# A two-block transformer kernel on one core: eight more modulation blocks are summed by VectorE, and output chunks are put ahead of the last transposings

## The reference

```python
m_lat = (jax.nn.silu(c) @ ada_w[i] + ada_b[i])[:, None, :]      # ada_w[i]: 1024 x 6144
m_ctx = jax.nn.silu(c_ctx) @ ada_w[i] + ada_b[i]
sh1, sc1, g1, sh2, sc2, g2 = jnp.split(m_lat, 6, axis=-1)
h = _rms(x, norm1_g[i]) * (1.0 + sc1) + sh1
o, oc = _even_mixer(h, hc, ...)      # in-projection, Fourier mix, window attention, out-projection
x = x + g1 * o
h = _rms(x, norm2_g[i]) * (1.0 + sc2) + sh2
x = x + g2 * _swiglu(h, ffn_w_gate[i], ffn_w_up[i], ffn_w_down[i])
```

## Time and profile before

| | us |
|---|---|
| median of 3 runs | 2134.99 (2134.18 to 2138.87) |
| the profiled execution | 2134.16 |
| its span in the profile | 2132.3 |
| PE busy in the span | 2070.2 (97%) |
| DVE busy | 1499.5 (70%) |
| ACT busy | 975.3 (46%) |
| POOL busy | 325.4 (15%) |

### The profile page before, as it was taken

How to read it: one execution, slowest core, us unless ns; L and a number is a source line. 1 busy time by engine, 2 the same in 40 slices (tenths; PEclk the granted TensorE clock), 3 DMA queues, 4 the chain that set the end, 5 groups by cost and what they waited for, 6 DMA issues and landing times.

```text
span 2132.3 us, 34735 instructions
## 1 busy us (share of the span) xinstructions
PE 2070.2 (97%) x12633; PEld 1770.0 (83%) x12633; DVE 1499.5 (70%) x2685; ACT 975.3 (46%) x1545; POOL 325.4 (15%) x340
## 2 busy tenths in 40 slices
PE   7999999999989998999999999999999999999998
PEld 3756778888878768999999989999988888888887
DVE  5535578894247855665687867997986677777776
ACT  3436332222234365444478534447743444444444
POOL 0114000000004031000000016887820000000000
PEclk9999999999999999999999999999999999999999
DMA  8351245694226303555545544551156655555553
GB/s 294 118 210 69 99 158 194 214 325 136 96 79 179 99 11 110 186 180 188 181 160 165 174 159 136 172 169 60 60 184 221 198 187 188 190 191 189 187 188 117
DMA packets 92896, 342.18 MB, mean 160 GB/s; under 512 B 10383, under 2 KB 10399, under 8 KB 92272
## 3 DMA queue, kind: packets, MB, share of 16 engines
q1 hardware_dynamic: 89280, 325.10, 45.5%
q0 software_dynamic: 3504, 15.56, 2.5%
HBM read 339.57 MB, written 1.05 MB: 160 GB/s over the span
## 4 chain that ended last, share of the span: by engine, by line
PE 91%; DVE 4%; ACT 2%; issue 1%; DMA 1%; POOL 1%; SPq 0%; DVEq 0%; ACTq 0%; POOLq 0%
PE banks L1077 20%; PE banks L1514 16%; PE banks L1126 9%; PE banks L1480 7%; PE banks L1392 6%; PE banks L1263 5%; PE banks L1483 3%; PE banks L1441 3%; PE banks L975 2%; PE banks L1425 2%; PE banks L1091 2%; PE banks L1165 2%; PE banks L957 1%; PE banks L1004 1%; PE banks L1018 1%
## 5 line engine op out<-in xcount | busy, mean ns | idle before, releaser
L1077 PE MATMUL banks<-act_parts,first_w_parts 128*128 128x512 f32 (+1 forms) x2544 | 464.4, 344 | 3.1 <-DVE ffn_hidden_parts L2121 1.7
L1077 PEld LDWEIGHTS banks<-act_parts,first_w_parts 128*128 128x128 f32 x2544 | 400.9, 190 | 63.9 <-issue 7.3
L1514 PE MATMUL banks<-w_parts,a_parts 128*128 128x512 f32 x1524 | 360.4, 390 | 0.1
L2121 DVE TENSOR_TENSOR first_w_parts<-weight_ring,first_w_parts 128x1024 fp32r<-128x1024 f32 x166 | 206.8, 1248 | 202.1 <-ACT first_w_parts L1708 202.0
L1514 PEld LDWEIGHTS banks<-w_parts,a_parts 128*128 128x128 f32 x1524 | 285.9, 188 | 59.5 <-issue 0.8
L2121 DVE TENSOR_TENSOR w_parts<-weight_ring,w_parts 128x1024 fp32r<-128x1024 f32 x207 | 253.7, 1226 | 74.3 <-ACT w_parts L1708 71.7
L1708 ACT ACTIVATE w_parts<-weight_ring 128x1024 fp32r<-128x1024 f32 x207 | 218.9, 1057 | 184.0 <-PE banks L1480 102.1
L1708 ACT ACTIVATE first_w_parts<-weight_ring 128x1024 fp32r<-128x1024 f32 x166 | 174.8, 1056 | 237.2 <-PE banks L1077 124.0
L1480 PE MATMUL banks<-n_parts,w_parts 128*128 128x512 f32 x632 | 229.4, 397 | 1.3 <-DVE w_parts L2121 1.3
L1126 PE MATMUL banks<-ffn_hidden_parts,first_w_parts 128*128 128x512 f32 (+1 forms) x1056 | 183.4, 336 | 0.0
L1126 PEld LDWEIGHTS banks<-ffn_hidden_parts,first_w_parts 128*128 128x128 f32 x1056 | 162.6, 190 | 20.5
(11 more groups left out here) (327 smaller groups left out, 2904.0 us busy)
## 6 DMA issues: line engine op xcount, KB each, us to landing
weight_ring<-in_stream SPq DMA_DIRECT2D x618, 512.0 KB, 3.3
main_zone<-in_rel_bias POOLq DMA_DIRECT2D x6, 512.0 KB, 11.7
rounded<-in_dft_input POOLq DMA_DIRECT2D x1, 1600.0 KB, 7.5
rounded<-in_dft_inverse POOLq DMA_DIRECT2D x1, 1280.0 KB, 7.8
main_zone<-in_xT POOLq DMA_DIRECT2D x1, 1024.0 KB, 11.5
main_zone<-in_ctxT POOLq DMA_DIRECT2D x1, 1024.0 KB, 16.2
main_zone<-in_c_rows POOLq DMA_DIRECT2D x1, 1024.0 KB, 8.4
tail_zone<-in_rel_bias POOLq DMA_DIRECT2D x2, 512.0 KB, 23.6
```

What stands on the lines that cost most here:

```text
L1077: mm = pe.matmul(o[:, 0:w], wb[:, hw, k, :], fin[:, hx, k, 0:w], start=(k == 0 and n == 0), stop=(k == DC - 1 and n == 2))
L1514: mm = pe.matmul(acc[n][:, :], ap_[:, e % 3, ha, (n // 2) * P:(n // 2 + 1) * P], wp[(B + b) % PARTS][:, hw, (n % 2) * 512:(n % 2 + 1) * 51 ...
L2121: return dve.tensor_tensor(o, a, b, op)
```

## The change

Row 4 of layer 0 moves from TensorE to VectorE. Its eight blocks (`MODS` 0 to 7, two samples each) are summed by `mod_sums` inside `qk_norm`: blocks 0 to 3 after the last normalised chunk and before the first sine product, blocks 4 to 7 one before each later sine product. `SOONER` places their loads among those of `ada0b`, which now has 16 blocks. The condition rows for them are two new loads by GpSimd, and two SiLU by ScalarE after the last square root of `qk_root`. TensorE does 3, 2 and 1 `ada` blocks around the filter products instead of 6, 1 and 1, the same ten in turns 3 to 7, and none in the attention. ScalarE's `ada_copy(1)` stands before the attention instead of in its fourth step. In both attentions `out_part` comes before `turn` in the last steps, with more chunks in each. All of SP's loads of this part are written out instead of partly looped.

```diff
-STREAM = [("ada0a", 16), ("ev_in", 10), ("ada0b", 24), ("ev_out", 8), ("ffn_gu0", 2 * FC), ("mods", 56), ...
+STREAM = [("ada0a", 16), ("ev_in", 10), ("ada0b", 16), ("ev_out", 8), ("ffn_gu0", 2 * FC), ("mods", 64), ...
-MODS = ([(0, 5, _j, 2) for _j in range(8)] + ...
+MODS = ([(0, 4, _j, 2) for _j in range(8)] + [(0, 5, _j, 2) for _j in range(8)] + ...
+SOONER = {5: (0, 1), 7: (2,), 9: (3,), 11: (4,), 13: (5,), 15: (6, 7)}
-_at = 0
+_at = 8
...
         ORDER.append((_n, _i))
+        if _n == "ada0b":
+            ORDER += [("mods", _b) for _b in SOONER.get(_i, ())]
...
+        c_sooner = [second_rows[:, D:2 * D], view(CSOON0, D)]
...
-                if KIND[last + 1][0]:
+                if KIND[last + 1][0] and name != "ada0b":
                     return tile_free, TILE[name] + dict(TILES)[name]
                 return blocks_used, n + 2
...
-            fill = [[(1, "ada0b", b, b // DC, b // DC == 0, b // DC == 2) for b in range(24)], []]
+            fill = [[(1, "ada0b", b, b // DC, b // DC == 0, b // DC == 1) for b in range(16)], []]
...
-                for f in fill[0][:6]:
+                for f in fill[0][:3]:
                     ada(*f)
                 filter_dft(0)
-                ada(*fill[0][6])
+                for f in fill[0][3:5]:
+                    ada(*f)
                 filter_dft(1)
-                ada(*fill[0][7])
+                ada(*fill[0][5])
...
-                        for f in fill[0][2 * u + 2:2 * u + 4]:
+                        for f in fill[0][2 * u:2 * u + 2]:
                             ada(*f)
...
+                    if i >= PAIRS:
+                        out_part(l, AHEAD_OF_VALUES[l][i - PAIRS])
                     if 0 <= i - 2 < PAIRS:
                         turn(i - 2)
-                    if i >= PAIRS:
-                        out_part(l, AHEAD_OF_VALUES[l][i - PAIRS])
...
-            AHEAD_OF_VALUES = [[(0,), (1,), (2,)], [(0,), (1, 2), (3,)]]
+            AHEAD_OF_VALUES = [[(0,), (1, 2), (3, 4)], [(0,), (1, 2, 3), (4, 5)]]
...
-                    if l == 0 and i == 3:
-                        ada_copy(1)
...
             qk_root(0, 4)
+            act.wait_ge(crow_in, 32)
+            for s in (1, 0):
+                act.activation(c_sooner[s], c_sooner[s], ACT.Silu).then_inc(crow_ready, 1)
             dft_copy(0)
...
             v_copy()
+            ada_copy(1)
             attention(0)
...
                         if b == 0:
-                            dve.wait_ge(crow_ready, 2 - n)
+                            dve.wait_ge(crow_ready, 2)
+                            dve.wait_ge(dft_ready, 2)
+                        if b == 8:
+                            dve.wait_ge(crow_ready, 4 - n)
+                        o, c = (view(CPROD0, D), c_sooner[1 - n]) if b < 8 else (twins[3][:, :], c_rows[:, 1 - n, :])
...
+                mod_sums(range(4))
                 for j, (c, w, g, sq_at, r_at) in enumerate(CHUNKS[0]):
+                    if j >= 1:
+                        mod_sums([3 + j])
                     dve.wait_ge(rot_ready, j + 1)
...
+            pool.dma_start(c_sooner[0], t["c_rows"][:, 0:D]).then_inc(crow_in, 16)
...
+            pool.wait_ge(filt_ready, 6)
+            pool.dma_start(c_sooner[1], t["c_rows"][:, D:2 * D]).then_inc(crow_in, 16)
```

More of the change, by code:

```diff
@@ L60 @@
 GROUP = 2
-STREAM = [("ada0a", 16), ("ev_in", 10), ("ada0b", 24), ("ev_out", 8), ("ffn_gu0", 2 * FC), ("mods", 56), ("ffn_d0", FC),
+STREAM = [("ada0a", 16), ("ev_in", 10), ("ada0b", 16), ("ev_out", 8), ("ffn_gu0", 2 * FC), ("mods", 64), ("ffn_d0", FC),
           ("od_in", 24), ("od_out", 8), ("ffn_gu1", 2 * FC), ("ffn_d1", FC),
@@ L67 @@
           ("peer", 2 * KEYS - DONE)]
-MODS = ([(0, 5, _j, 2) for _j in range(8)] + [(1, _r, _j, 2) for _r in range(2) for _j in range(8)]
+MODS = ([(0, 4, _j, 2) for _j in range(8)] + [(0, 5, _j, 2) for _j in range(8)] + [(1, _r, _j, 2) for _r in range(2) for _j in range(8)]
         + [(1, _r, _j, 1) for _r in range(2, 6) for _j in range(8)])
 MODS_AT = {}
-_at = 0
+SOONER = {5: (0, 1), 7: (2,), 9: (3,), 11: (4,), 13: (5,), 15: (6, 7)}
+_at = 8
 for _m in range(1, 20):
@@ L255 @@
 CROWS0 = 21504
+CSOON0, CPROD0 = 25600, 19456
 HALF0 = FS0 + 2048
@@ L688, in release @@
                     return extra_ready, i + 1
-                if name in ("ada0a", "ada0b") and KIND[last + 1][0]:
+                if name in ("ada0a", "ada0b") and i == dict(STREAM)[name] - 1:
                     return ada_rows, 1 + ("ada0a", "ada0b").index(name)
-                if KIND[last + 1][0]:
+                if KIND[last + 1][0] and name != "ada0b":
                     return tile_free, TILE[name] + dict(TILES)[name]
@@ L792, in ada_turn @@
             def ada_turn(phase):
[L794 removed]
+                nj = 2
                 pe.wait_ge(ada_rows_copied, 2 * (phase + 1))
```

17 lines of the change are left out of this document (9 added, 8 removed).

## The result

| | before | with the change |
|---|---|---|
| median of 6 runs each, us | 2136.1 (2134.18 to 2139.2) | 2146.77 (2143.84 to 2155.79) |
| ratio, 95% interval | | 1.0051, 1.0039 to 1.0062 |
| profiled execution, span | 2134.16, 2132.3 | 2148.81, 2146.9 |

The kernel is slower by 10.7 us, where 4.8 was forecast. The direction was right (it had a chance of 0.50, against 0.46 for no change), the size was not: 2146.77 is above the range, which ended at 2143.0.

What follows compares the result with a forecast made beforehand. TensorE, 91% of the chain, was taken as the bound, with VectorE's late sums delaying the attention. +5.4 - 1.0 - 0.7 - 0.2 + 1.3 = +4.8 us took the median from 2134.99 to 2139.8, range 2134.5 to 2143.0.

Steps and rivals of the forecast that it cites:

- Prelude, -0.8: Fourier stage, filter products: fewer TensorE blocks around them, so turn 0 starts 0.8 us earlier, at 116.0 instead of 116.78.
- Ring: Fourier stage: blocks arrive through one ring in order, so VectorE's sums land late and rotations of chunks 2 and 4 wait.
- Lock, "nothing on the sum": First VectorE sum: locked beside GpSimd's cosine product, it takes about 6.6 us, adding nothing to the total.
- The last landings: End of Fourier stage: m6 lands at 145.2, VectorE's addition ends at 154.7, attention opens at 155.5 after 4.0 us idle TensorE.
- The stage's term: Fourier stage to first scores: attention opens at 155.5 instead of 150.09, +5.4 us, between -0.8 and about +8.
- Out-projection, -0.7 and -0.2: Ends of both attentions: out-projection chunks fill waits at the transposings, -0.7 us in the first, -0.2 in the second.
- Attention without fill, -1.0: First attention's start: without ada blocks the transposing ends at 157.0, saving 1.0 us, bounds 0 and 1.58.
- the clock, +1.3: First attention: the 4.0 us wait before it brings a fall of TensorE's clock, +1.3 us, between 0 and 2.6.
- At nothing: SiLU with table load, two GpSimd loads, ada_copy(1) and one more small addition: costed at nothing.
- At no term at all: Start of the program to the Fourier stage: the prediction had no term for it, forecast 0.
- two falls of the clock: Rival, Fourier turns 4 and 5: stalls lower the clock, delaying a10 and a12, 3 us more, 2143; chance 0.12.
- VectorE keeps up: Rival, Fourier stage: m3 lands by 129.0, VectorE is as early as TensorE, -2.7 us, 2132.3; chance 0.11.

Runs made afterwards that it cites:

- 2: The change without row 4's eight loads, VectorE making its sixteen full sums from data already in SBUF (row 4 not computed): 2136.75 us, ratio 1.0000.
- 3: The change without early sums and without their loads, one small copy instead (row 4 not computed): 2136.88 us, ratio 1.0004 to the kernel before.
- Experiment 8: The change with GpSimd's cosine product delayed until three blocks are summed: one run, 2142.78 us.
- 7: The kernel before with only the out-projection's part: out_part ahead of turn and the new AHEAD_OF_VALUES: 2137.43 us, ratio 1.0007.
- 6: The change with the unused matmuls of 4 and the useless fill of 5, row 4 computed: one run, 2141.71 us.
- 5: As 3, with six blocks' worth of useless 32-column matmuls in the attention's first three steps: 2137.4 us, ratio 1.0006 to the kernel before.
- 4: The change with four unused fp32 matmuls on TensorE after the turning of the values: 2144.24 us, ratio 1.0041 to the kernel before.
- 12: As 11 without the wait of Experiment 8, the cosine product cut into five, each made once its chunk is normalised: 2132.4 us, ratio 0.9980.
- experiment 1: The change with its sixteen early sums over 64 of 1024 columns, all loads kept: 2141.02 us, ratio 1.0015 to the kernel before.
- 9: The change with each ada0b block counted as used at its own last matmul: one run, 2140.35 us.
- 11: The change with the edits of Experiment 8 and 9, six blocks back in the attention's first steps, row 4's loads sooner: 2133.9 us, ratio 0.9991.

## Why the prediction was right in direction and short in size

I take its steps in their order; times after are put back by the 3.5 us with which that execution entered the stage.

- **Prelude, -0.8.** Right: 43.1 against 43.9 in 2 and 3, and 9.75 us from the stage's start to turn 0 with the change, against 10.61.
- **Ring.** Right in its mechanism and nearly in its steps. m3's sum starts at 130.9 (forecast 130.3), the rotation of chunk 2 at 134.3 (133.6), m5's sum at 140.9 (m5 to land at 140.5), the rotation of chunk 4 at 144.3 (143.8).
- **Lock, "nothing on the sum".** Right in length (6.49 against 6.6), wrong in its price. I had SP's issue of m3 follow a9's at once. But that load waits until m1 has been used, and m1's sums were held up by the lock: SP issued a9 at 128.04 and m3 only at 129.00, both in that profile's own time. Experiment 8 gives the lock 1.5 us in all.
- **The last landings.** m6's sum starts at 147.1, forecast 145.2: a15, m6 and m7 were issued at 144.50, 144.88 and 145.35 in that profile's own time (m6 0.6 us later than forecast, once put back), and their median landing took 5.7 us, where the forecast had given m6 4.4 from its issue. Together: first scores at 157.1, forecast 155.5, and a wait of 4.70 against 4.0. The stage's term was +5.4 and measured +7.0.
- **Out-projection, -0.7 and -0.2.** The first was right (-0.6). The second was wrong in sign (+0.2). The step had seen that fewer chunks are left behind the last values (0.3 us of waiting in 7), but not the wait of 0.5 for the row minima before the first chunk. How the rest comes about is not shown.
- **Attention without fill, -1.0, and the clock, +1.3.** This is the step that failed. I costed the blocks as work that TensorE loses, and looked for falls of the clock only where a long wait stood. The blocks also kept TensorE busy between scores that wait for row minima. Without them the clock fell with waits under 0.9 us (3), and the stall made the stretch longer. Against 57.6 (6) and 57.4 (5) the attention of the change took 62.4: the clock's term is about +5, not +1.3. (Counted from the kernel before: +3.5 in all, less the -0.6 of the chunks and the -1.0 to 0 of the fill, is +4.1 to +5.1.) Of it the missing fill costs 1.0 to 3.0 by itself (2 and 3 against 5: the same instructions in the attention and the same waits up to the fall, but 6.8 and 10.2 us at the low clock). The stall's part is the 2.0 to 4.0 from there to 62.4; by 4 it is 3.3. Whether -1.0 would come if the clock stayed up is open: no run had the clock at 1.00 without fill.
- **At nothing.** Nothing speaks against it: the two SiLU, the loads and `ada_copy(1)` show no wait of TensorE on them. The stretch from 54.68 (58.16) to the Fourier stage is 51.49 us with the two new loads and without. 3, which keeps all of them, is no longer in its Fourier stage than forecast, and 5 and 6 have `ada_copy(1)` ahead of the attention and the shortest attentions but that of 12.
- **At no term at all.** The first stretch of the table, +3.5 in these two profiles, whose cause is open.

The Trainium skill, "TensorE: Matmul & The Clock Gate", section "HAM oscillation — how this bites in real kernels", counts the low time times (1 - 1.2/2.4), so half of it as lost. The early stretch agrees: 3.4 us more at the low clock cost 1.6 there, between 38 and 50 us. In the attention the runs differ from it: 17.1 us more than in 6 cost 4.8, 0.3 us for each and not 0.5. That TensorE often waits for other engines there would explain it, but that is not shown. My +1.3 for some 4 us had the price per us about right; it was short because the clock was low for 20.5 us in all, in three stretches. The Trainium skill, "SBUF — State Buffer", section "SBUF: two separate sides", says that whichever operation starts first has the ports for its whole instruction and the other waits. The trace agrees, at 128 x 64 too (5.50 us beside a product of 5.60 that had begun before it, experiment 1).

Of the rivals, "two falls of the clock" was the nearest in its number (2143), which is luck, since its mechanism did not come: no fall came in turns 4 and 5, where the waits were 0.5 and 1.0 us. "VectorE keeps up" had the right condition: in 12, where no landing is late, it does, and the change's idea then pays, with the fill left in the attention and the cosine product cut.

## What to carry to other kernels

Work that fills a stage bound by latency has two values: the time it takes, and the clock it holds for the small matmuls around it. Before taking it away, look at the granted clock of that stage and at how busy the engine would be without it, not only at its waits. When an engine gets work that hangs on loads, follow the ring in its own order of issue; the sums by themselves cost nothing here (2), and 5.5 of the stage's 7.0 us came back when the places in the ring were freed sooner (9).

## What the runs showed of the hardware that I had not expected

- The granted clock fell to 0.50 around 155 us with no wait over 0.88 us, in a stretch of dependent scores (3); six blocks' worth of 32-column matmuls that nobody reads kept it at 1.00 (5). Behind a stall of 2.58 us such fill did not prevent the fall (11).
- A microsecond at 0.50 cost this attention about 0.3 us (3 against 5, the change against 6, 7 against 12), and the stretch of 38 to 50 us nearly 0.5.
- A sum of 64 columns took 5.50 us beside a GpSimd product of 5.60, alone 0.22: what is paid is GpSimd's remaining time, so cutting the VectorE operation doesn't help and cutting GpSimd's does (five pieces; the longest sum 2.05 us).
- Two `ada` blocks side by side cost 1.07 us and a block alone 1.05, so a load 0.2 us late costs over 1 us when it splits a pair (1).
